# First scan: the remainders of 27 filler weight tiles on VectorE instead of GpSimd, their rounding some units ahead

## The chip, the cores and the metric

One core of one Trainium2 chip runs the whole program. The metric is the device time in microseconds (us) of one execution. In the text TensorE is PE in the profile, VectorE is DVE, ScalarE is ACT, GpSimd is POOL and SyncE is SP (its DMA queue SPq).

## What is computed

One inference step of one hybrid decoder layer: 2048 prompt tokens, 32 sample tokens, width 1024. In the part that matters here, normalised rows go through the input weight (1024 x 3072), and the pieces of the result feed a recurrence (HGRN2) in chunks and a gated chunk mixer:

```python
z = hn @ w_in
zq, zf, zi, zg, zu, zv = jnp.split(z, ...)
f = lb + (1.0 - lb) * jax.nn.sigmoid(zf32)
k = (1.0 - lb) * jax.nn.sigmoid(-zf32)
S_new, o = hgrn2_scan(S0, q, k, logf, v)        # per chunk, 4 heads
o_hg = rmsnorm_per_head(o) * jax.nn.sigmoid(zg)
u = jax.nn.gelu(zu)
vn = layernorm(jax.nn.gelu(zv), ln_v_g, ln_v_b)
o_cm = chunk_gmlp(u, vn, w_s, b_s)
x = x + jnp.concatenate([o_hg, o_cm], axis=-1) @ w_out
```

Cross-attention to 256 memory tokens and an MLP of width 4096 follow. All is float32.

## The kernel before

**Products.** A float32 product is made of three products of a rounded type (fp32r): each operand is split into a rounded part (`hi`) and a remainder (`lo`), and `gemm` (line 946) issues lo x hi, hi x lo and hi x hi. Activations are split by ScalarE (`a_hi`) and VectorE (`a_lo`), weights tile by tile.

**Blocks.** The prompt runs in four blocks of 512 tokens, "first" to "last". Weights come in tiles of 128x512 through a ring of RING = 8 pairs (`w_ring`: `w_hi`, `w_lo`). In the first block a tile is loaded raw (`w_raw`, RAW = 4 slots), split on the core, used, and its pair is stored to `w_pairs` in DRAM. The later blocks load ready pairs and split nothing. In the first block GpSimd splits most tiles by itself, two instructions each: rounding (line 864) and remainder (line 867), in `split`.

**The scan.** Tiles 0 to 23 of a block are zf, zi, zq. Then eight units (four chunks, two pairs of heads each) follow one another. For a unit u, TensorE issues the level products (`within_chunk`, line 1087), some tiles' products of zv, zg and zu as filler (`fill`, FILL = 5 ahead of the units, then 3, 2, 3, 2, 4, 3, 2), and the output and state products (`rows_and_state`, lines 1111 to 1113). Tiles 24 to 31 are zv, 32 to 39 zg, 40 to 47 zu, and 48 to 55 the first half of w_out, used behind the scan; two of these are used ahead of the transposes "oto" (line 954 in the profile), six behind them. After unit 6 come the chunk mixer's products "mix" (line 1155), which need zu's GELU and free halves of PSUM. PSUM is two halves of four banks; every job has one, and `begin` waits until the job before in that half is evacuated. zg and the outputs of units 4 to 7 share a half.

VectorE's order for unit u: `attention(u)` (needs the level products), `new_state(u - 1)` (line 2287), `args(u + 2)` (line 2238), `scaled(u + 1)` (end factors line 2246, then seven level products line 2251, which release `ends_ready` and `scaled_ready` for TensorE), then pieces of the layer norm by unit: statistics behind unit 1, scale behind unit 2, `lng_row` behind 3, `lnb_row` behind 4, `gate` behind 5, `uu` behind 6. In the first block `mixed_rows` stands behind all units, in the others behind unit 6; "oto" waits for the mixed rows.

ScalarE's order for unit u: `decays(u + 2)` (exponentials, lines 1640 to 1643), GELU of zv at u = 0, sigmoid of zg at u = 4 (SWAP, ahead of `decays(6)`), GELU of zu at u = 6 (all line 1708), the copies of the unit's output (`unit_out`), small square roots at u = 1 and 5, and then `filler_tiles(u)`. A change between kinds of function costs a table load (line 1431).

**Filler tiles.** FILLERS = (29, 56): the tiles 29 to 55 are rounded by ScalarE in `filler_tiles` (line 1673), at places given by FILLER_HI, and GpSimd makes each remainder (line 883) when its rounding is done. ScalarE waits, for tile i, for the store of the pair i - 8, the raw load of i, and TensorE's use of tile i - 8:

```python
act.wait_ge(w_stored[i % RING].sem, i // RING * 16 + 16)
act.wait_ge(w_in[i % RAW].sem, i // RAW * 16 + 16)
act.wait_ge(w_used.sem, W_TILES["mem"] + i + 1)
nc.scalar.copy(w_hi[:, i % RING, :], w_raw[:, i % RAW, :]).then_inc(filler_hi, 1)
```

**SyncE.** `load` (line 613) issues, tile after tile, the raw load of tile i (line 622) once the remainder of tile i - 4 is made (`w_split`), and then the store of pair i - 4 (line 604). `block_loads` (line 708) orders them: the six pieces of w_in (tiles 0 to 47), in the first block then `first_sample_loads` (49 small loads for the sample requests, lines 773 to 781, and two of 2 MB, line 757), then w_out's first half (tiles 48 to 55), a wait for unit 7's attention, the rows of x, and w_out's second half from tile 56 on.

The functions that the diff touches are printed below.

Of the kernel before, what the change touches and what calls it, by code (L numbers as in the profile page):

```python
# [17 lines left out]
ALU = mybir.AluOpType  # L18
# [34 lines left out]
FILL = (5, 3, 2, 3, 2, 4, 3, 2)  # L53

FILLERS = (29, 56)
FILLER_HI = {"zq": range(29, 33), "kt": range(33, 34), 0: range(34, 38), 1: range(38, 42), 2: range(42, 45), 3: range(45, 47), 4: range(47, 48),
             5: range(48, 52), 6: range(52, 56)}

SG = NS + DS
SLV = 3  # L60
# [146 lines left out]
def program(nc, I, O):  # L207
# [14 lines left out]
    with ctx:  # L222
# [630 lines left out]
        @block.gpsimd  # L853
        def _(pool):
            pool.sem_inc(w_split.sem, RAW)
            nc.gpsimd.memset(zero[:], 0.0).then_inc(w_rounded, 1)
            pool.wait_ge(w_rounded, 1)
            def split(g, k, n, tile0, by_act):

                s = k % RAW  # L860
                pool.wait_ge(w_stored[k].sem, g * 16 + (n // RING * 16 + 16))
                pool.wait_ge(w_in[s].sem, g * (16 * RING // RAW) + (n // RAW * 16 + 16 * (k // RAW + 1)))
                pool.wait_ge(w_used.sem, g * RING + (W_TILES["mem"] + tile0 + k + 1))
                nc.gpsimd.tensor_tensor(w_hi[:, k, :], w_raw[:, s, :], zero[:].to_broadcast([P, 512]),  # L864
                                        ALU.add).then_inc(w_rounded, 1)
                pool.wait_ge(w_rounded, g * RING + (n - by_act + k + 2))
                nc.gpsimd.tensor_tensor(w_lo[:, k, :], w_raw[:, s, :], w_hi[:, k, :].bitcast(F32),  # L867
                                        ALU.subtract).then_inc(w_split.sem, 1)

            for s in range(RING):  # L870
                pool.sem_inc(w_stored[s].sem, 16)
            first, after = FILLERS
            with pool.Fori(0, first // RING) as g:
                for k in range(RING):
                    if k % 4 == 0:
                        pool.wait_ge(*done("mem", ("nv", 5 if k == 0 else 7)))
                    split(g, k, 0, 0, 0)
            for i in range(first // RING * RING, first):
                split(0, i % RING, i // RING * RING, i // RING * RING, 0)
            for i in range(first, after):  # L880

                pool.wait_ge(filler_hi, i - first + 1)
                nc.gpsimd.tensor_tensor(w_lo[:, i % RING, :], w_raw[:, i % RAW, :], w_hi[:, i % RING, :].bitcast(F32),
                                        ALU.subtract).then_inc(w_split.sem, 1)
            with pool.Fori(0, (FOLD0 - after) // RING) as g:
                for k in range(RING):
                    split(g, k, after, after, after - first)
            with pool.Fori(0, (W_TILES["first"] - FOLD1) // RING) as g:
                for k in range(RING):
                    split(g, k, FOLD0, FOLD1, after - first)  # L890
# [533 lines left out]
        def _(act):  # L1424
# [207 lines left out]
            def block_scalar(pos, b, last):  # L1632
# [68 lines left out]
                for u in range(UNITS):  # L1701
                    if u + 2 < UNITS and u != SWAP:
                        decays(u + 2)
                    for at, name, dst in ((0, "zv", vn), (SWAP, "zg", gate), (6, "zu", uu)):
                        if u == at:
                            tables("sigmoid_and_others" if name == "zg" else "gelu_apprx_tanh_and_others")
                            act.wait_ge(*done(pos, name))
                            nc.scalar.activation(dst[:], out_of(pos, name)[:], ACT.Sigmoid if name == "zg" else
                                                 ACT.Gelu_apprx_tanh).then_inc(evacuated_of(pos, name), 1)
                    if u == SWAP:  # L1710
                        decays(u + 2)
                    if u == UNITS - 1:
                        round_hi_halves(pos, "otu", a_hi[:, 4:8, :])
                    unit_out(u)
                    if u == 1:
                        rsqrt(pos, "ln", TT)
                    if u == 5:
                        rsqrt(pos, "oa", 12)
                    filler_tiles(u)
                rsqrt(pos, "ob", 4)  # L1720
                round_hi(pos, "oto", a_hi[:, 0:4, :], out_of(pos, "oto")[:])
# [88 lines left out]
        def _(dve):  # L1810
# [420 lines left out]
            def block_vector(pos, last):  # L2231
# [11 lines left out]
                def scaled(u):  # L2243
# [7 lines left out]
                        ins = nc.vector.tensor_tensor(v, v, signed(kq, u, w), ALU.mult)  # L2251
                    ins.then_inc(scaled_ready.sem, 1)

                def attention(u):


                    ps = levels_of(pos, u)
                    wide = ps[:, 2, 0:2 * P].rearrange("p (j t) -> p j t", j=2)
                    v = ps[:, 3, 0:GROUP_LEVELS * 2 * GROUP].rearrange("p (a e j t) -> p a e j t", a=3, e=2, j=2)

                    def own_size(i, n=1):

                        return masks[:, i:i + n, None, 0:GROUP].bitcast(mybir.dt.int32).to_broadcast([P, n, 2, GROUP])

                    nc.vector.tensor_copy(yt[:, 36:37], ident[:, 0:1])
                    nc.vector.copy_predicated(v[:, :, 0], own_size(0, 3), v[:, :, 1]).then_inc(dve_sem, 1)
                    nc.vector.copy_predicated(att[:], masks[:, 5:6, :].bitcast(mybir.dt.int32).to_broadcast([P, 2, P]), wide)
                    dve.wait_ge(dve_sem, link.next())
                    nc.vector.tensor_copy(yt[:, 36:37], ident[:, 0:1])
                    nc.vector.copy_predicated(v[:, 0:1, 0], own_size(4), v[:, 1:2, 0]).then_inc(dve_sem, 1)  # L2270
                    dve.wait_ge(dve_sem, link.next())
                    nc.vector.tensor_copy(yt[:, 36:37], ident[:, 0:1])
                    nc.vector.copy_predicated(v[:, 0:1, 0], own_size(6), v[:, 2:3, 0]).then_inc(dve_sem, 1)
                    dve.wait_ge(dve_sem, link.next())
                    nc.vector.tensor_copy(yt[:, 36:37], ident[:, 0:1])
                    groups = [P, 2, P // GROUP, GROUP]
                    nc.vector.copy_predicated(att[:].rearrange("p j (g t) -> p j g t", t=GROUP),
                                              masks[:, 3:4, :].bitcast(mybir.dt.int32).rearrange(
                                                  "p j (g t) -> p j g t", t=GROUP).to_broadcast(groups),
                                              v[:, 0, 0, :, None, :].to_broadcast(groups)).then_inc(att_ready.sem, 1)  # L2280
# [43 lines left out]
                    "p h (c t) -> p h c t", c=TT), ALU.mult).then_inc(evacuated_of(pos, "zq"), 1)  # L2324
                dve.wait_ge(*out(pos, "zq"))
                scaled(0)
                for u in range(UNITS):
                    dve.wait_ge(levels_done.sem, levels_done.at(pos, u))
                    attention(u)
# [3 lines left out]
                        args(u + 2)  # L2333
                    if u + 1 < UNITS:
                        scaled(u + 1)
                    if u == 1:

                        dve.wait_ge(*out(pos, "zv"))
                        for t in range(TT):
                            ins = nc.vector.bn_stats(stats[:, t, :], vn[:, t, :])  # L2340
                        ins.then_inc(dve_sem, 1)
                        dve.wait_ge(dve_sem, link.next())
                        nc.vector.tensor_copy(yt[:, 36:37], stats[:, TT - 1, 0:1])
                        for t in range(TT):
                            ins = nc.vector.bn_aggr(mv[:, t, :], stats[:, t, :])
                        ins.then_inc(dve_sem, 1)
                        dve.wait_ge(dve_sem, link.next())
                        nc.vector.tensor_scalar(var[:, 16:16 + TT], mv[:, :, 1], EPS, None, ALU.add
                                                ).then_inc(var_ready.sem, 1)
# [26 lines left out]
                    if u == 6:  # L2376
                        dve.wait_ge(*out(pos, "zu"))
                        ps = out_of(pos, "mix")
                        for g in range(H):
                            c = slice(g * P, g * P + P)  # L2380
                            dve.wait_ge(mix_done.sem, mix_done.at(pos, g))
                            nc.vector.scalar_tensor_tensor(uu[:, :, c], ps[:, g, :].rearrange("p (t c) -> p t c", c=P),
                                                           bs_col[:, g:g + 1], uu[:, :, c], ALU.add, ALU.mult
                                                           ).then_inc(uu_ready.sem if g < H - 1 else
                                                                      evacuated_of(pos, "mix"), 1)
                if pos == "first":
                    mixed_rows()
                dve.wait_ge(o_ready.sem, o_ready.at(pos, UNITS - 1))
# [188 lines left out]
```

## Time and profile before

| | us |
|---|---|
| median of 3 runs | 2933.81 |
| lowest, highest | 2933.69, 2934.37 |
| profiled execution, its time | 2933.21 |
| profiled execution, its span | 2931.4 |
| TensorE busy | 2886.1 (98%) |
| weight loads (PEld) | 2334.1 (80%) |
| VectorE busy | 1251.3 (43%) |
| ScalarE busy | 642.9 (22%) |
| GpSimd busy | 440.9 (15%) |

The span runs from the first instruction to the last of the profiled execution; its time has 1.8 us around it. Shares of busy time are means over the whole span: the scans of the four blocks are short parts of it, in which the other engines set the pace at places. Times in the rows are counted from the span's start.

### The profile page before, as it was taken

Reading aid. Unit: us, or ns where it says so; the run is one execution under the profiler, and the core shown is the slowest. Engines: PE = TensorE matmul, PEld = TensorE weight load, DVE = VectorE, ACT = ScalarE, POOL = GpSimd, SP = SyncE. Lnnn points to the kernel's source line nnn. Section 1 sums busy time; section 2 is a strip of 40 time slices with the busy share of each in tenths; the row PEclk is TensorE's granted clock in tenths of the full one; section 3 lists DMA queues with packets and bytes.
Section 4 is the critical chain, followed back from the end, with each engine's and each line's share of the span. In section 5 each row is a group of like instructions: output and inputs, shape, how many; then the busy total and the mean of one; then the engine's idle time right before and its main releaser. Section 6 shows DMA issues by size and latency. Waiting matters only on the chain.

```text
span 2931.4 us, 40394 instructions
## 1 busy us (share of the span) xinstructions
PE 2886.1 (98%) x17243; PEld 2334.1 (80%) x17243; DVE 1251.3 (43%) x2096; ACT 642.9 (22%) x999; POOL 440.9 (15%) x362
## 2 busy tenths in 40 slices
PE   8998999999999999999999999999999999999998
PEld 7787787777888888788788888877778888877787
DVE  5578443453344733322243744222234473322233
ACT  4435221110123411111122422101012341211011
POOL 0182408788810000000000000000000000000000
PEclk9999999999999999999999999999999999999999
DMA  8895757989975455665666445566767545567654
GB/s 311 311 324 187 278 188 279 361 288 310 329 255 174 154 185 204 222 231 199 223 215 223 142 176 185 199 250 250 274 236 273 178 155 187 180 226 286 235 193 150
DMA packets 207677, 675.93 MB, mean 231 GB/s; under 512 B 22864, under 2 KB 28240, under 8 KB 207504
## 3 DMA queue, kind: packets, MB, share of 16 engines
q1 hardware_dynamic: 200480, 662.72, 63.3%
q10 hardware_dynamic: 7024, 10.68, 1.0%
q8 instruction: 136, 2.23, 0.3%
q14 instruction: 37, 0.30, 0.0%
HBM read 542.84 MB, written 130.48 MB: 230 GB/s over the span
## 4 chain that ended last, share of the span: by engine, by line
PE 89%; DVE 6%; SPq 1%; DMA 1%; ACT 1%; issue 0%; POOL 0%; ACTq 0%; DVEq 0%
PE half L946 81%; PE half L954 2%; PE half L1275 2%; DVE lvl L2238 1%; PE half L1087 1%; PE half L963 1%; DVE lvl L2251 1%; PE half L1155 1%; DMA w_raw<-in_w_out 0%; PE half L1285 0%; DMA mem_raw<-in_w_ck 0%; SPq L599 0%; DMA w_pairs<-stage 0%; DVE state L2287 0%; SPq L779 0%
## 5 line engine op out<-in xcount | busy, mean ns | idle before, releaser
L946 PE MATMUL half<-a_hi,w_ring 128*128 128x512 f32 x2560 | 822.6, 397 | 0.0
L946 PE MATMUL half<-w_ring,a_hi 128*128 128x512 f32 x2176 | 677.1, 392 | 0.0
L946 PE MATMUL half<-w_ring,ht_hi 128*128 128x512 f32 x2016 | 626.5, 392 | 0.0
L946 PEld LDWEIGHTS half<-a_hi,w_ring 128*128 128x128 f32 x2560 | 480.2, 188 | 131.6 <-issue 14.3
L946 PE MATMUL half<-a_lo,w_ring 128*128 128x512 f32 x1280 | 505.4, 395 | 0.0
L946 PEld LDWEIGHTS half<-w_ring,a_hi 128*128 128x128 f32 x2176 | 410.3, 189 | 90.0
L946 PEld LDWEIGHTS half<-w_ring,ht_hi 128*128 128x128 f32 x2016 | 378.9, 188 | 82.2
L946 PE MATMUL half<-w_ring,a_lo 128*128 128x512 f32 x1088 | 433.6, 399 | 5.1 <-DVE a_lo L1839 3.6
L946 PE MATMUL half<-w_ring,ht_lo 128*128 128x512 f32 x1008 | 395.5, 392 | 0.8 <-DVE ht_lo L2464 0.8
L2472 DVE SCALAR_TENSOR_TENSOR x<-half,rstd,x 128x512 f32<-128x512 f32 x252 | 171.7, 744 | 300.7 <-PE half L946 300.7
L946 PEld LDWEIGHTS half<-a_lo,w_ring 128*128 128x128 f32 x1280 | 240.2, 188 | 56.2
L946 PEld LDWEIGHTS half<-w_ring,a_lo 128*128 128x128 f32 x1088 | 205.3, 189 | 51.4 <-issue 5.4
L864 POOL TENSOR_TENSOR w_ring<-w_raw,zero 128x512 fp32r<-128x512 f32 x165 | 184.3, 1117 | 295.9 <-DMA w_raw<-in_w_up 129.0
L867 POOL TENSOR_TENSOR w_ring<-w_raw,w_ring 128x512 fp32r<-128x512 f32 x165 | 224.3, 1360 | 12.9
L946 PEld LDWEIGHTS half<-w_ring,ht_lo 128*128 128x128 f32 x1008 | 189.4, 188 | 44.3 <-DVE ht_lo L2464 1.3
L1760 ACT ACTIVATE relu<-half 128x2048 f32<-128x2048 f32 x32 | 60.3, 1883 | 660.5 <-PE half L946 654.4
L2461 DVE TENSOR_TENSOR relu<-relu,half 128x2048 f32<-128x2048 f32 x32 | 73.2, 2287 | 292.6 <-ACT relu L1760 292.6
L946 PE MATMUL half<-w_ring,b_hi 128*128 128x512 f32 x512 | 158.9, 392 | 0.0
L1461 ACT ACTIVATE a_hi<-half 128x2048 fp32r<-128x2048 f32 (+1 forms) x30 | 54.8, 1825 | 439.7 <-PE half L954 439.7
L1839 DVE TENSOR_TENSOR a_lo<-half,a_hi 128x2048 fp32r<-128x2048 f32 (+1 forms) x30 | 66.6, 2220 | 197.6 <-ACT a_hi L1461 197.6
L946 PEld LDWEIGHTS half<-w_ring,b_hi 128*128 128x128 f32 x512 | 96.2, 188 | 21.1
L2464 DVE TENSOR_TENSOR ht_lo<-relu,ht_hi 128x2048 fp32r<-128x2048 f32 x32 | 75.9, 2372 | 63.2 <-ACT ht_hi L1762 63.2
(309 smaller groups left out, 2473.6 us busy)
## 6 DMA issues: line engine op xcount, KB each, us to landing
w_ring<-w_pairs SPq DMA_DIRECT2D x704, 512.0 KB, 3.2
w_pairs<-w_ring SPq DMA_DIRECT2D x192, 512.0 KB, 5.0
w_pairs<-stage SPq DMA_DIRECT2D x16, 1024.0 KB, 6.0
w_raw<-in_w_up SPq DMA_DIRECT2D x64, 256.0 KB, 4.5
w_raw<-in_w_down SPq DMA_DIRECT2D x64, 256.0 KB, 3.9
w_s<-in_w_up SPq DMA_DIRECT2D x8, 2048.0 KB, 11.1
w_s<-in_w_down SPq DMA_DIRECT2D x8, 2048.0 KB, 11.5
w_raw<-in_w_in SPq DMA_DIRECT2D x48, 256.0 KB, 4.3
```

The source lines that it names most:

```text
L864: nc.gpsimd.tensor_tensor(w_hi[:, k, :], w_raw[:, s, :], zero[:].to_broadcast([P, 512]), ALU.add).then_inc(w_rounded, 1)
L867: nc.gpsimd.tensor_tensor(w_lo[:, k, :], w_raw[:, s, :], w_hi[:, k, :].bitcast(F32), ALU.subtract).then_inc(w_split.sem, 1)
L946: m = nc.tensor.matmul(ps[:, j, :], l, r, start=(i == 0 and q == 0), stop=(i == tiles_in - 1 and q == 2))
L954: m = nc.tensor.transpose(ps[:, bank0 + i // 4, (i % 4) * P:(i % 4) * P + P], t, ident[:])
L963: m = nc.tensor.matmul(out, l, r, start=(first and i == 0), stop=(last and i == 2))
L1275: m = nc.tensor.matmul(ps[rows, 0, :], src[:, k, :], w_s[k // 4][:, k % 4, c * 512:c * 512 + 512], start=(k < 2), stop=(k >= KD - 2))
L1461: nc.scalar.activation(dst, src, ACT.Copy, scale=scale).then_inc(hi_ready.sem, 1)
L1760: nc.scalar.activation(relu[:], out_of(pos, ("up", e))[:], ACT.Relu).then_inc(relu_ready.sem, 1)
L1839: ins = nc.vector.tensor_tensor(dst, src, hi.bitcast(F32), ALU.subtract)
L2461: nc.vector.tensor_tensor(relu[:], relu[:], out_of(pos, ("up", e))[:], ALU.mult).then_inc(sq_ready.sem, 1)
L2464: nc.vector.tensor_tensor(ht_lo[e % 2][:], relu[:], ht_hi[e % 2][:].bitcast(F32), ALU.subtract).then_inc(evacuated_of(pos, ("up", e)), 1)
L2472: ins = nc.vector.scalar_tensor_tensor(xc, out_of(pos, ("dn", e, c))[:, t, :], rstd[:, 24 + t:25 + t], xc, ALU.mult, ALU.add)
```

## The change

The remainders of the tiles 29 to 55 are made by VectorE, in eight groups (FILLER_LO): one behind scaled(0), one behind each scaled(1) to scaled(6), and the last behind all units, ahead of `mixed_rows`. GpSimd waits until they are made, and goes on with tile 56. FILLER_HI has ScalarE round the tiles at earlier places: 33 to 36 ahead of unit 0, then behind the units 0 to 5 37-39, 40-43, 44-45, 46-48, 49-51 and 52-55. The table for GELU is loaded behind unit 5's square root. SyncE's program is not changed.

```diff
-FILLER_HI = {"zq": range(29, 33), "kt": range(33, 34), 0: range(34, 38), 1: range(38, 42), 2: range(42, 45), 3: range(45, 47), 4: range(47, 48),
-             5: range(48, 52), 6: range(52, 56)}
+FILLER_HI = {"zq": range(29, 33), "kt": range(33, 37), 0: range(37, 40), 1: range(40, 44), 2: range(44, 46), 3: range(46, 49),
+             4: range(49, 52), 5: range(52, 56)}
+FILLER_LO = ((29, 33), (33, 37), (37, 40), (40, 44), (44, 46), (46, 49), (49, 52), (52, 56))
...
-            for i in range(first, after):
-
-                pool.wait_ge(filler_hi, i - first + 1)
-                nc.gpsimd.tensor_tensor(w_lo[:, i % RING, :], w_raw[:, i % RAW, :], w_hi[:, i % RING, :].bitcast(F32),
-                                        ALU.subtract).then_inc(w_split.sem, 1)
+            pool.wait_ge(w_split.sem, w_split.at("first", after - 1))
...
                     if u == 5:
                         rsqrt(pos, "oa", 12)
+                        tables("gelu_apprx_tanh_and_others")
                     filler_tiles(u)
...
+                def remainders(turn):
+
+                    for i in range(*FILLER_LO[turn]) if pos == "first" else ():
+                        dve.wait_ge(filler_hi, i - FILLERS[0] + 1)
+                        if i == FILLERS[0]:
+                            dve.wait_ge(w_split.sem, w_split.at(pos, i - 1))
+                        nc.vector.tensor_tensor(w_lo[:, i % RING, :], w_raw[:, i % RAW, :], w_hi[:, i % RING, :].bitcast(F32),
+                                                ALU.subtract).then_inc(w_split.sem, 1)
...
                 scaled(0)
+                remainders(0)
                 for u in range(UNITS):
...
                     if u + 1 < UNITS:
                         scaled(u + 1)
+                        if u + 1 < UNITS - 1:
+                            remainders(u + 1)
...
+                remainders(UNITS - 1)
                 if pos == "first":
                     mixed_rows()
```

## Rows read from the trace of the kernel before

**Rows 1.** Windows table, both scans: us, PE, PEld, DVE, ACT, POOL busy, PEclk, DMA, GB/s

```profile
215.60:278.50 62.90, 54.34 (x785) 44.66 (x785) 56.84 (x147) 36.49 (x76) 18.93 (x14) 0.97 0.48 169
278.50:313.90 35.40, 31.63 (x499) 27.72 (x497) 26.59 (x65) 18.13 (x41) 12.09 (x9) 0.95 0.80 303
...
2318.20:2372.00 53.80, 52.37 (x786) 43.58 (x785) 47.55 (x147) 29.24 (x62) 0.00 (x0) 1.00 0.40 138
2372.00:2402.80 30.80, 30.14 (x500) 26.28 (x499) 25.09 (x79) 12.97 (x32) 0.00 (x0) 1.00 0.32 113
```

**Rows 2.** The timeline of TensorE, first block: start us, us, instruction xcount [idle before]

```profile
303.75 5.31 PE L1155 MATMUL half<-vn,ws_t 128*128 128x128 f32 x32 [3.66 <-ACT uu L1708]
...
321.62 1.97 PE L954 MATMUL half<-ident,vv 128*128 128x128 f32 x16 [1.91 <-DVE vv L2295]
```

**Rows 3.** The timeline of TensorE, last block

```profile
2394.10 3.81 PE L1155 MATMUL half<-vn,ws_t 128*128 128x128 f32 x32 [0.50 <-ACT uu L1708]
...
2408.39 1.91 PE L954 MATMUL half<-ident,vv 128*128 128x128 f32 x16
```

**Rows 4.** The waits of TensorE, 215 to 325 us: total, times, longest

```profile
PE half L1111 <- issue: 3.8, 2, 2.3
...
PE half L1111 <- DVE ends L2246: 3.5, 1, 3.5
```

**Rows 5.** VectorE's groups by shape, first block's scan (207.8 to 321.7 us)

```profile
L2251 DVE TENSOR_TENSOR lvl<-lvl,kq 128x256 f32<-128x256 f32 x56 | 27.7, 561 | 0.0
L2238 DVE TENSOR_TENSOR lvl<-bn 128x256 f32<-128x256 f32 x42 | 19.4, 530 | 0.0
L2287 DVE SCALAR_TENSOR_TENSOR state<-state,e_last,added 128x128 f32<-128x128 f32 x16 | 10.4, 690 | 0.0
```

**Rows 6.** VectorE's groups by shape, last block's scan (2308.6 to 2408.5 us)

```profile
L2251 DVE TENSOR_TENSOR lvl<-lvl,kq 128x256 f32<-128x256 f32 x56 | 20.1, 432 | 0.0
L2238 DVE TENSOR_TENSOR lvl<-bn 128x256 f32<-128x256 f32 x42 | 15.0, 431 | 0.0
...
L2287 DVE SCALAR_TENSOR_TENSOR state<-state,e_last,added 128x128 f32<-128x128 f32 x16 | 4.9, 346 | 0.4 <-ACT osq L1663 0.4
```

**Rows 7.** Line 883 on GpSimd: durations ns min/median/max, first and last start

```profile
L883 POOL TENSOR_TENSOR w_ring<-w_raw,w_ring x27: 1267/1337/1692, 208.7 to 309.4; 128x512 fp32r<-128x512 f32 x27
```

**Rows 8.** The timeline of SyncE's queue, 258 to 280 us

```profile
258.98 0.33 SPq L622 DMA_DIRECT2D w_raw<-in_w_in  x1
...
278.74 0.95 SPq L757 DMA_DIRECT2D w_s<-in_w_in  x2
...
279.74 0.50 SPq L622 DMA_DIRECT2D w_raw<-in_w_out  x1
```

**Rows 9.** DMA issues at 278.74 and 279.74: KB each, us from issue to landing

```profile
w_s<-in_w_in SPq DMA_DIRECT2D x2, 2048.0 KB, 11.6
...
w_raw<-in_w_out SPq DMA_DIRECT2D x1, 256.0 KB, 14.5
```

**Rows 10.** The timeline of ScalarE, first block's scan

```profile
267.20 1.13 ACT L1673 CAST w_ring<-w_raw 128x512 fp32r<-128x512 f32 x2
...
270.46 1.89 ACT L1708 ACTIVATE gate<-half 128x2048 f32<-128x2048 f32 x1 [0.83 <-PE half L946]
...
294.28 0.63 ACT L1673 CAST w_ring<-w_raw 128x512 fp32r<-128x512 f32 x1 [0.30 <-DMA w_raw<-in_w_out]
...
300.43 1.28 ACT L1431 ACT_TABLE_LOAD   x1
```

**Rows 11.** The timeline of VectorE, first block, unit 6's scalings

```profile
296.62 0.68 DVE L2246 TENSOR_TENSOR ends<-ends,kq 128x512 f32<-128x512 f32 x1
297.22 5.75 DVE L2251 TENSOR_TENSOR lvl<-lvl,kq 128x256 f32<-128x256 f32 x7
```

**Rows 12.** The timeline of VectorE, last block, behind attention(2)

```profile
2343.35 0.61 DVE L2287 SCALAR_TENSOR_TENSOR state<-state,e_last,added 128x128 f32<-128x128 f32 x2
...
2346.90 2.51 DVE L2251 TENSOR_TENSOR lvl<-lvl,kq 128x256 f32<-128x256 f32 x7
```

## The prediction

> **What bounds the kernel now.** I read the page first: TensorE is busy for 98% of the span, so only its idle and slow-clock stretches can give time back or grow. The change touches the first block's scan alone, so I set that scan beside the last block's, which issues the same products with weights already split and has no filler tiles. The windows table cuts both at the same places: unit 0's level products, unit 4's output products, the first w_out product [rows 1]. The first block takes 62.9 and 35.4 us, the last 53.8 and 30.8: 13.7 us lost. To the transposes of "oto" it is 321.62 - 215.6 = 106.0 against 2408.39 - 2318.2 = 90.2, so 15.8 us is all that a perfect cure could return [rows 1, 2, 3]. The reader should see in rows 2 how the late part is lost: "mix" waits 3.66 us for ACT's GELU of zu and then runs 5.31 us where the last block's takes 3.81 after a 0.50 us gap; the granted clock averages 0.95 in that stretch, that is, a part of it ran at 1.2 GHz instead of 2.4. So a gap of some 3.5 us costs another 1.5 us behind it.
>
> The early part is lost on DVE [rows 4]: TensorE waits 3.5 us for the second unit's end factors and 3.8 us where the profile names nobody. The DVE groups by shape show why: scalings, arguments and state updates take 27.7, 19.4 and 10.4 us here, 20.1, 15.0 and 4.9 in the last block [rows 5, 6]. That is 17.5 us more for the same 114 instructions, and GpSimd's 27 remainders, 1.337 us each, run between them [rows 7].
>
> The third reading decides. SyncE issues tile 47's load at 258.98, as soon as GpSimd has the remainder of 43. Then come all the sample requests' small loads and two 2 MB loads (278.74), and only then tile 48, the first of w_out (279.74) [rows 8]. It lands 14.5 us after its issue, behind the 4 MB [rows 9]. ACT rounds it at 294.28, having waited for that DMA [rows 10]. From the remainder of 43 to the rounding of 48 is 294.28 - 258.98 = 35.3 us, and nothing in it depends on who makes remainders.
>
> **The change, part by part.** *Remainders leave GpSimd*: the 17.5 us of slowed DVE work go. *They come to DVE*: 27 of 128x512. The nearest DVE row is the end factors' 128x512 product, 296.62 to the next start at 297.22, 0.60 us [rows 11]; bounds are 0.36 (2.51 / 7, for half the size [rows 12]) and GpSimd's 1.337 [rows 7]. I take 0.60, as both its inputs lie in SBUF too: 27 x 0.60 = 16.2 us. On DVE's books the exchange is nearly even, 17.5 for 16.2. The Trainium skill (SBUF — State Buffer, "Who interferes with whom") says that a DVE instruction with two SBUF inputs blocks against a GpSimd one that reads SBUF; Perfetto Trace Analysis, "Optimizing Scalar/DVE Operations", also of the Trainium skill, adds that moving work between those two "might not help". Rows 5 to 7 agree with the first; the second alone would forecast about no change, and is my second case below.
>
> Turns 0 and 1 lie in DVE's wait for level products and cost nothing; without that cover they would cost 4 x 0.60 = 2.4 us each. Turns 2 and 3 lie ahead of attention(2) and of attention(3), where DVE is what TensorE waits for.
>
> *ACT rounds earlier*: FILLER_HI now has 46, 47 and 48 behind unit 3's output, where it had 45 and 46. SyncE's order is unchanged, so tile 48 still needs its 35.3 us after the remainder of 43. When is that? In the last block attention(2) is over at 2343.35, and scaled(3)'s seven products start at 2346.90 and take 2.51 [rows 12]: over at 2349.4, in the first block's time (2318.2 - 215.6 = 2102.6 less) 246.8. Add turn 2 (three tiles, 1.8, ahead of attention(2)) and turn 3 (four, 2.4): the remainder of 43 is ready at 251.0, 8.0 us sooner than the 258.98 of now. Tile 48 then can be rounded at 294.28 - 8.0 = 286.3. ACT reaches it after unit 3's output, near 266 to 268 (its casts of 45 and 46 start at 267.20 now [rows 10]). It waits there about 19 us, and its queue is in order.
>
> *What is queued behind that wait*: the sigmoid of zg, decays(6), unit 4's copies. TensorE's unit 4 output products write the half that zg holds, so they wait for this sigmoid. After the last cast the table load and the sigmoid take 270.46 + 1.89 - (267.20 + 1.13) = 4.0, less the 0.8 waited for TensorE, 3.2 us [rows 10]. So 286.3 + 0.6 + 3.2 = 290.1, against 278.5 now [rows 1]: **+11.6 us**. DVE waits too, for tile 48 in turn 5, with the addition of lnb_row and attention(5) behind it; both are wanted only after unit 4's output, so that costs nothing more. TensorE itself would be ready near 269.4 + 1.8 + 2.4 = 273.6, so it idles some 16 us. The earlier stretches' gains and losses all end in this gap.
>
> *From there to the first w_out product*: the w_out tiles now have long landed, so no GELU wait: the last block's 30.8, plus 0.6 because the cast of 55 needs the slot freed by TensorE's last filler product and stands ahead of zu's GELU, plus 1.5 for the slow clock behind the long gap: 32.9 against 35.4, **-2.5 us**. The GELU table load moved into unit 5 costs nothing: it runs ahead of ACT's wait for TensorE's last filler product; uncovered it is 1.28 us [rows 10].
>
> *To the "oto" transposes*: before, 321.62 - 313.9 = 7.7 us, 1.91 of it waiting for DVE's mixed rows [rows 2]. Turn 7 now stands ahead of those rows: 4 x 0.60 = 2.4 us in full. The gap becomes 4.3 us, long enough for another 1.5 us at the lower clock: **+3.9 us**.
>
> Tile 56's load now waits for the remainder of 52, and GpSimd's own splitting with it. Tile 56 is wanted six tiles after "oto"; two tiles take 7.7 - 1.9 = 5.8 us, so that is 17 us on, and a delay of 3 us stays hidden. Behind the scan the first block has no TensorE wait that could take back a shift, so it reaches the end whole.
>
> **Sum**: 11.6 - 2.5 + 3.9 = +13.0 us. The profiled execution took 2933.21, so 2946.2; the median of the three runs is 0.6 above it, so I forecast 2946.8. The only size that a page prices differently is the landing: by SBUF — State Buffer of the Trainium skill, "The DMA setup-cost knee", a transfer is about 2 us plus bytes at 436 GB/s, 12.2 us for the 4.46 MB from 278.74 on; the rows show 15.5 (294.28 - 278.74), so the page would make the sum some 3 us smaller, and the trace decides.
>
> **Rivals.** *A, forecast: tile 48 stalls ACT.* For it: an unchanged SyncE program and a measured 35.3 us. *B, not slower: the landing does not gate.* If tile 48 lands before 273.6 - 3.8 = 269.8, ACT's wait costs nothing. That needs 19 us instead of 35.3, for example if the small loads issued far faster than their 20 us or the 4 MB didn't stand ahead; the change is even already where the 35.3 are 13.0 less, 22.3. Then: the last block's 90.2, plus turns 2 to 4 in DVE's way (nine tiles, 5.4), 0.6 for the cast of 55, 2.4 for turn 7, about 2.0 because the first block's mixed rows stand behind unit 7, 1.5 of clock: 102.1 against 106.0, -3.9, 2929.9. *C, faster: B, and the remainders all fit into DVE's idle time*: the full 15.8, 2918.0. Against it: turn 7 sits right on the path. *D, a longer stall*: each DVE remainder at 1.0 us moves tile 48 by 7 x 0.4 = 2.8, and the clock stays low longer: 2951 to 2953. *E, DVE is not freed* because its slow instructions come from elsewhere than GpSimd: the 17.5 us are 2.2 a unit, so three units bring the remainder of 43, and the stall, 6.6 later: 2953.4. Rows 5 and 6 speak against it.
>
> **How the numbers follow.** A with D and E 0.87, B 0.10, C 0.03. 0.2% is 5.9 us, about what a measurement tells from no change. A and its variants lie above it at all but the low end, B within, C beyond: slower 0.86, same 0.11, faster 0.03. Range: down 8.2 for a landing 2 us sooner, no clock cost (3.0), half of turn 7 hidden (1.2) and 2 more for an earlier remainder of 43; up 6.3 by D and E: 2938.6 to 2953.1.
>
> **What would show it.** Right: one TensorE gap of about 16 us at unit 4's output products released by ACT's gate; an ACT idle of about 19 us ahead of one cast, released by the DMA of in_w_out; scaled lvl products at 432 ns mean; a GELU gap at "mix" under 2 us; a gap of some 4 us ahead of "oto"; no GpSimd work between 205 us and the first tile of the next group. Wrong: tile 48's cast without a wait, or DVE products still above 500 ns.

## The result: 20 us slower, and the profile after

| | before | after |
|---|---|---|
| median (runs) | 2934.09 (4) | 2954.22 (4) |
| lowest, highest | 2933.69, 2935.55 | 2953.15, 2957.27 |
| ratio, 95% interval | | 1.0067 [1.0055, 1.008] |
| profiled execution, time and span | 2933.21, 2931.4 | 2953.15, 2951.4 |
| TensorE, VectorE, GpSimd busy | 2886.1, 1251.3, 440.9 | 2888.0, 1253.4, 405.9 |

The changed kernel is slower, as forecast, by 20.1 us where 13.0 were forecast; its median lies 1.1 us above the upper end of the range. The busy sums tell nothing of it: TensorE's and VectorE's hardly moved. The waits do. This is the table of TensorE's waits in the changed kernel, 215 to 345 us (total, times, longest), which answers to [rows 4]:

```profile
PE half L1108 <- ACT gate L1705: 18.4, 1, 18.4
PE half L951 <- DVE vv L2302: 7.9, 1, 7.9
PE half L1108 <- DVE ends L2244: 3.2, 1, 3.2
PE half L1152 <- ACT uu L1705: 1.1, 1, 1.1
```

One gap of 18.4 us stands at unit 4's output products (line 1108), released by the sigmoid that reads zg. A second of 7.9 us stands ahead of "oto" (line 951), where [rows 2] had 1.91. The wait for GELU at "mix" fell from 3.66 to 1.10. The changed kernel's windows table, cut at the places of [rows 1], with a third stretch from the first w_out product to "oto":

```profile
215.40:293.30 77.90, 54.77 (x786) 44.86 (x785) 57.23 (x163) 34.42 (x73) 0.00 (x0) 0.89 0.62 227
293.30:326.20 32.90, 31.61 (x499) 27.74 (x499) 23.57 (x67) 20.65 (x46) 0.00 (x0) 0.95 0.35 125
326.20:339.80 13.60, 5.72 (x24) 4.37 (x24) 12.86 (x30) 3.00 (x9) 4.56 (x4) 0.78 0.99 369
```

The first stretch has 77.9 us instead of 62.9 with the same products, the second 32.9 instead of 35.4, the third 13.6 instead of 7.7. The column behind ACT, GpSimd's, holds nothing for two stretches and four instructions in the third: these four matter below.

Next, the cause of the large gap. ScalarE's timeline in the changed kernel (start us, us, instruction, idle before it):

```profile
266.42 0.62 ACT L1670 CAST w_ring<-w_raw 128x512 fp32r<-128x512 f32 x1 [2.16 <-PE half L943]
289.36 0.62 ACT L1670 CAST w_ring<-w_raw 128x512 fp32r<-128x512 f32 x1 [22.32 <-DMA w_raw<-in_w_out]
290.00 1.28 ACT L1428 ACT_TABLE_LOAD   x1
291.29 1.88 ACT L1705 ACTIVATE gate<-half 128x2048 f32<-128x2048 f32 x1
```

The cast of tile 48, now the third behind unit 3's output, waits 22.32 us for its load; the table load and zg's sigmoid stand behind it in the queue, and TensorE goes on at 293.31, when the sigmoid is over. Now why the load is late: SyncE's queue in the changed kernel,

```profile
249.07 0.33 SPq L623 DMA_DIRECT2D w_raw<-in_w_in  x1
...
250.40 1.01 SPq L605 DMA_DIRECT2D w_pairs<-w_ring  x1
251.46 0.50 SPq L623 DMA_DIRECT2D w_raw<-in_w_in  x1
252.00 1.15 SPq L605 DMA_DIRECT2D w_pairs<-w_ring  x1
253.19 0.64 SPq L623 DMA_DIRECT2D w_raw<-in_w_in  x1
253.87 1.19 SPq L605 DMA_DIRECT2D w_pairs<-w_ring  x1
255.09 0.89 SPq L774 DMA_DIRECT2D own<-in_c_own  x1
...
274.74 0.95 SPq L758 DMA_DIRECT2D w_s<-in_w_in  x2
275.74 0.50 SPq L623 DMA_DIRECT2D w_raw<-in_w_out  x1
```

and the same place in the kernel before:

```profile
258.98 0.33 SPq L622 DMA_DIRECT2D w_raw<-in_w_in  x1
259.35 0.73 SPq L604 DMA_DIRECT2D w_pairs<-w_ring  x1
260.12 0.46 SPq L773 DMA_DIRECT2D own<-in_c_own  x1
```

One line of VectorE's timeline of the changed kernel shows when the four remainders 40 to 43 were made:

```profile
248.37 2.49 DVE L2258 TENSOR_TENSOR w_ring<-w_raw,w_ring 128x512 fp32r<-128x512 f32 x4
```

They are over by 250.86 (248.37 + 2.49), but the load of tile 47 is issued at 253.19 and the first sample load at 255.09. The four remainders arrive 0.6 us apart; each lets SyncE issue a load and a store, and its eight DMAs take 6.0 us. From the remainder of 43 to the first sample load it is 4.23 us, where it was 1.14 (260.12 - 258.98). The sample loads and the two of 2 MB then take 20.65 us (19.62 before), and tile 48 is cast 13.62 us behind its issue (14.54 before): 38.5 us in all, where [rows 8, 10] gave 35.3. Of the 3.2 more, 3.1 stand in that first part, 1.0 in the small loads, and the landing is 0.9 shorter.

VectorE was freed as said. Its groups by shape in the changed kernel, first block's scan, which answer to [rows 5] and [rows 6]:

```profile
L2249 DVE TENSOR_TENSOR lvl<-lvl,kq 128x256 f32<-128x256 f32 x56 | 20.0, 428 | 0.0
L2258 DVE TENSOR_TENSOR w_ring<-w_raw,w_ring 128x512 fp32r<-128x512 f32 x27 | 17.0, 683 | 16.6 <-ACT w_ring L1670 16.6
L2236 DVE TENSOR_TENSOR lvl<-bn 128x256 f32<-128x256 f32 x42 | 15.0, 431 | 0.0
```

The 56 scalings take 20.0 us instead of 27.7, the 42 arguments 15.0 instead of 19.4: the last block's figures. The new 27 remainders take 17.0. VectorE's 16.6 us of idleness is its own wait for tile 48, and costs nothing more.

Last, the gap at "oto". VectorE in the changed kernel:

```profile
334.44 1.00 DVE L1824 SCALAR_TENSOR_TENSOR yt<-y 128x4 f32<-128x4 f32 x1 [0.51 <-ACT y L1438]
335.48 0.16 DVE L1827 TENSOR_TENSOR yt<-yt,var 128x4 f32<-128x4 f32 x1
335.68 1.11 DVE L1829 SCALAR_TENSOR_TENSOR rstd<-yt,y 128x4 f32<-128x4 f32 x1
336.83 2.96 DVE L2302 SCALAR_TENSOR_TENSOR vv<-vv,rstd,gate 128x128 f32<-128x128 f32 x4
```

VectorE in the kernel before, the same instructions:

```profile
319.84 0.16 DVE L1826 SCALAR_TENSOR_TENSOR yt<-y 128x4 f32<-128x4 f32 x1 [0.51 <-ACT y L1441]
...
320.43 1.14 DVE L2295 SCALAR_TENSOR_TENSOR vv<-vv,rstd,gate 128x128 f32<-128x128 f32 x4
```

Two of the three little ones take 1.00 and 1.11 us instead of 0.16, and the four products 2.96 instead of 1.14. What runs beside them is GpSimd, in the changed kernel:

```profile
334.39 1.04 POOL L865 TENSOR_TENSOR w_ring<-w_raw,zero 128x512 fp32r<-128x512 f32 x1 [129.77 <-DMA w_raw<-in_w_out]
335.50 1.27 POOL L868 TENSOR_TENSOR w_ring<-w_raw,w_ring 128x512 fp32r<-128x512 f32 x1
```

and in the kernel before:

```profile
322.60 1.04 POOL L864 TENSOR_TENSOR w_ring<-w_raw,zero 128x512 fp32r<-128x512 f32 x1 [11.91 <-DMA w_raw<-in_w_out]
```

Before, GpSimd took up tile 56 at 322.60, when the mixed rows were made (320.43 + 1.14 = 321.57). After, turn 7 has pushed the mixed rows back by 2.5 us, while tile 56 comes in nearly as early: 8.2 us behind the first w_out product (334.39 - 326.17) against 8.6 (322.60 - 313.96). They meet.

### The profile page after: what moved, and what is told of

It is laid out like the page before. It is cut to its first block, busy times and chain, and to the rows that moved or that the text cites. A ratio compares the mean times of both kernels' runs of the same rounds, so it can differ in the third digit from the quotient of the medians.

```text
span 2951.4 us, 40395 instructions
## 1 busy us (share of the span) xinstructions
PE 2888.0 (98%) x17243; PEld 2335.9 (79%) x17243; DVE 1253.4 (42%) x2123; ACT 643.3 (22%) x999; POOL 405.9 (14%) x335
## 4 chain that ended last, share of the span: by engine, by line
PE 89%; DVE 6%; DMA 2%; SPq 1%; ACT 1%; issue 0%; ACTq 0%; DVEq 0%
PE half L943 80%; PE half L951 2%; PE half L1272 2%; DVE lvl L2249 1%; DVE lvl L2236 1%; PE half L1084 1%; PE half L960 1%; DMA w_raw<-in_w_out 1%; PE half L1152 1%; PE half L1282 0%; DMA mem_raw<-in_w_ck 0%; SPq L600 0%; SPq L780 0%; DVE stats L2350 0%; DMA w_pairs<-stage 0%
```

## The experiments

The profiled executions differ by up to 4 us ahead of the first block's scan, which the change doesn't touch. So besides the time each has a *stretch*: from unit 0's key transposes (starts 213.1 to 217.0) to the first product of the sample requests' part (line 1272 of the changed kernel). It is 494.06 - 215.32 = 278.7 us before and 514.28 - 215.17 = 299.1 after: 20.4 of difference, the whole change. Behind that point the two kernels take the same time to 0.2 us (2437.3 and 2437.1 of their spans); the kernels of the experiments take 2436.3 to 2441.0, with no edit there, so a difference of this size in a span is no effect of an edit. Each stretch is read from one execution, and a single time is weaker still: next to the experiments 5 to 8 the kernel before ran once too, and took 2940.60, 6.5 us over its usual median. What is said below of the experiments 1, 2 and 5 to 8 therefore rests on their stretches and rows, and nothing on a stretch's last microsecond.

**1. Tile 48 alone one place later.** The changed kernel, with its cast and remainder behind unit 4's output.

```diff
-FILLER_HI = {... 3: range(46, 49), 4: range(49, 52), 5: range(52, 56)}
-FILLER_LO = (... (46, 49), (49, 52), (52, 56))
+FILLER_HI = {... 3: range(46, 48), 4: range(48, 52), 5: range(52, 56)}
+FILLER_LO = (... (46, 48), (48, 52), (52, 56))
```

> The changed kernel with one place of one tile undone: tile 48 is rounded behind unit 4's output instead of unit 3's, and its remainder goes from VectorE's turn 5 to turn 6. Theory (ScalarE, in order, holds zg's sigmoid behind the cast of tile 48): the cast still starts near 289.4, released by the DMA of in_w_out, but zg's sigmoid runs near 271, so the wait of 18.4 us ahead of unit 4's output products is gone and those products start near 275. ScalarE's wait now stands behind unit 4 and holds decays(7) and unit 5's copies, so TensorE loses a part again ahead of unit 6's output products (6 to 8 us). The span falls by 8 to 11 us from 2951.4, to 2941 to 2944. Rival (VectorE, with 27 remainders more, is what TensorE waits for): the gap stays at 12 us or more, released by VectorE, and the span falls by less than 3 us.

Measured: 2944.71 in one run, stretch 289.1, 10.1 us less than after. TensorE's waits:

```profile
PE half L1108 <- DVE ends L2244: 12.2, 2, 9.0
```

The gap at unit 4 is gone, so it is tile 48's place that makes it. But the load is no earlier: the cast waits until 291.89, now with decays(7) queued behind, and 9.0 us of gap return at unit 6's output, where 6 to 8 were expected. Moving a wait down a queue gave back half of it.

**2. GpSimd held until the mixed rows are made.** The changed kernel with one wait more:

```diff
             pool.wait_ge(w_split.sem, w_split.at("first", after - 1))
+            pool.wait_ge(mixed_ready.sem, mixed_ready.at("first", TT - 1))
```

> The changed kernel, with GpSimd held from tile 56 on until the mixed rows are done. Theory (the mixed rows of the changed kernel run into GpSimd's resumed splitting): the last four updates of the mixed rows take 1.1 us in sum as in the kernel before, not 2.96, the two small steps ahead of them 0.16 each instead of 1.0 and 1.1, and the gap ahead of the oto transposes falls from 7.9 to 4.3 us; the span falls by 3.6 us, to about 2948, up to 2 us more if the clock then stays at its upper level. Rival (the gap is long because VectorE's own queue is longer: remainders and rows): the gap stays within 1 us of 7.9 and the span within 1 us.

Measured: 2949.79 in one run, stretch 296.1 (3.0 less, where the gap alone is 3.6 shorter). VectorE's timeline of this kernel ahead of "oto", and then TensorE's at it:

```profile
335.62 1.14 DVE L2303 SCALAR_TENSOR_TENSOR vv<-vv,rstd,gate 128x128 f32<-128x128 f32 x4
```

```profile
336.82 1.54 PE L952 MATMUL half<-ident,vv 128*128 128x128 f32 x6 [4.31 <-DVE vv L2303]
```

With GpSimd out of the way the products take 1.14 again and the gap is 4.31 us, the prediction's 4.3. The other 3.6 us of the gap are the collision.

**3 and 4. The sample requests' loads behind w_out's first half**, in the changed kernel (3) and in the kernel before (4).

```diff
-                if pos == "first":
-                    first_sample_loads()
                 load(pos, 6 * KD, I["w_out"][0], 0, 0, (4, 5, 6, 7, 0, 1, 2, 3))
+                if pos == "first":
+                    first_sample_loads()
```

> The changed kernel, with the sample requests' loads (49 small ones and the two of 2 MB) issued behind the loads of the tiles 48 to 55 instead of ahead of them. Theory (those loads set the time of tile 48): ScalarE waits for tile 48 at most 2 us, TensorE's gap at unit 4's output products is under 1 us, they start near 275, and the span falls by 17 to 19 us, to 2932 to 2935. Rival (VectorE is the bound behind it): TensorE still waits 4 us or more in the units 4 to 6, now for VectorE, and the span stays above 2938.

> The kernel before, with the same move of the sample requests' loads. Theory: the wait of 3.7 us ahead of the mixer's products for the GELU of zu, and the 1.5 us at the lower clock behind it, go, since tile 48 no longer keeps ScalarE; the span falls from 2931.4 by 3 to 5 us, to 2926.5 to 2928.5. Rival (the loads only move their price to the rows of x and the second half of w_out, which then come 10 us later): TensorE waits for those tiles or the sum with x, and the span rises by 2 us or more.

Measured for 3: median 2930.74 of 10 runs against 2935.04 of 16 of the kernel before, ratio 0.9985 [0.9975, 0.9994]; stretch 275.7, 23.4 less than after, more than the 17 to 19 expected. In ScalarE's timeline of this kernel tile 48's cast now waits for TensorE, for the 2.5 us that any filler cast there waits:

```profile
271.36 0.62 ACT L1670 CAST w_ring<-w_raw 128x512 fp32r<-128x512 f32 x1 [2.47 <-PE half L943]
```

TensorE's waits have no line for the gate any more, and "oto" leads them:

```profile
PE half L951 <- DVE vv L2302: 4.3, 1, 4.3
```

GpSimd takes up tile 56 at 332.64, 14.6 us behind the mixed rows (over at 318.06), since its load is now queued behind the sample loads: the collision is gone too, without the wait of experiment 2. The collision's 3.6 us are a part that the expectation had left out.

Measured for 4: median 2942.05 of 7 runs, ratio 1.0024 [1.0013, 1.0036], that is 7.0 us more; stretch 289.0, 10.2 more than before's one profiled execution. The wait at "mix" is gone as hoped, but see TensorE's waits and GpSimd's timeline of this kernel:

```profile
PE half L946 <- POOL w_ring L867: 10.2, 1, 10.2
```

```profile
298.89 1.73 POOL L883 TENSOR_TENSOR w_ring<-w_raw,w_ring 128x512 fp32r<-128x512 f32 x1
...
342.33 1.04 POOL L864 TENSOR_TENSOR w_ring<-w_raw,zero 128x512 fp32r<-128x512 f32 x1 [33.29 <-DMA w_raw<-in_w_out]
```

GpSimd makes the last remainder that w_out's first half waits for at 300.6 (298.89 + 1.73). Only then can the 49 small loads and the 4 MB be issued, from 302.57 on; tile 56 follows at 326.53, and TensorE waits 10.2 us for it behind "oto". Up to "oto" kernel 4 is 2.6 us ahead of the kernel before (103.7 against 106.3 from the key transposes); behind it it loses 12.8, these 10.2 and what the granted clock of 0.50 from 342.00 to 352.00 adds. In kernel 3 the small loads begin at 292.08 and tile 56's load is issued at 315.79. So the same edit of SyncE's order pays with the changed kernel's earlier fillers and costs with the old ones; I had expected a gain in both.

**5. The new places alone, GpSimd still makes the remainders**: the kernel before with the change's FILLER_HI and its table load behind unit 5's square root, nothing else.

> The kernel before with the rounding places (and the GELU table place) of the change alone; GpSimd still makes all 27 remainders. Theory (the loss is in when ScalarE meets tile 48, not in who makes remainders): ScalarE waits 15 us or more for the DMA of in_w_out ahead of the cast of tile 48, TensorE waits 12 to 16 us ahead of unit 4's output products for zg's sigmoid, which start at 287 to 291, and the span rises from 2931.4 by 7 to 12 us, to 2938 to 2943. Rival (the remainders on VectorE make the loss, by burdening the engine that TensorE waits for): no gap over 4 us in the scan, and the span stays within 2 us of 2931.4.

Measured: 2948.62 in one run, stretch 290.8 (12.0 more than before). TensorE's waits:

```profile
PE half L1111 <- ACT gate L1708: 12.1, 1, 12.1
PE half L1111 <- DVE ends L2247: 5.1, 1, 5.1
PE half L954 <- DVE vv L2296: 1.9, 1, 1.9
```

The gate's gap is there with GpSimd's remainders: the stall, and 12.0 of the 20.4 us, belong to where the tiles are rounded, not to who subtracts. The other 8.4 come only with the remainders on VectorE: from the key transposes to unit 4's output products it is 75.3 us here and 78.1 after, from there to "oto" 41.4 and 46.5, behind it 174.1 and 174.4. Here the "oto" gap is the old 1.9. Two lines, of SyncE and of ScalarE in this kernel, explain the first 2.9:

```profile
253.17 0.82 SPq L622 DMA_DIRECT2D w_raw<-in_w_in  x1
```

```profile
287.81 0.62 ACT L1673 CAST w_ring<-w_raw 128x512 fp32r<-128x512 f32 x1 [15.61 <-DMA w_raw<-in_w_out]
```

GpSimd, at 1.3 us and more for each, lets the load of tile 47 go at 253.17, with the first small load 1.37 us behind it, and tile 48 is cast 34.6 us later: about the 35.3 of the kernel before, and not the 38.5 of the changed one. From the key transposes its remainder of 43 is 1.0 us later than VectorE's (36.7 against 35.7), and tile 48's cast is still 2.9 earlier (71.3 against 74.2). The span rose by 15.4, 3.4 us more than the stretch, and past the 2938 to 2943 expected; 1.2 of them lie ahead of the stretch (216.47 for 215.32), and 2.2 behind its end, inside the spread given above.

**6. Only the two 2 MB loads moved**, in the changed kernel, behind w_out's first half; the 49 small ones stay.

```diff
 def first_sample_loads(): ...
-                load_product("zqf")
 ...
                 load(pos, 6 * KD, I["w_out"][0], 0, 0, (4, 5, 6, 7, 0, 1, 2, 3))
+                if pos == "first":
+                    load_product("zqf")
```

> The changed kernel with only the two 2 MB loads issued behind the loads of the tiles 48 to 55; the small ones stay where they are. Theory (of the 38.4 us between tile 43's remainder and tile 48's rounding about 24 are SyncE's issuing and the rest is landing behind 4 MB): tile 48's load is issued near 274.7 as before and lands 3 us later, its cast starts near 278, and the gap ahead of unit 4's output products is 6 to 8 us instead of 18.4; the span falls by 9 to 12 us, to 2939.5 to 2942.5. Rival (the 4 MB are all of it, the issue overlaps): the cast starts before 270 and the gap is gone. Rival (the small loads keep the DMA rings as busy as the large ones): the cast stays near 289.

Measured: 2940.96 in one run, stretch 288.4 (10.7 less than after). ScalarE and SyncE of this kernel:

```profile
276.15 0.62 ACT L1671 CAST w_ring<-w_raw 128x512 fp32r<-128x512 f32 x1 [11.23 <-DMA w_raw<-in_w_out]
```

```profile
272.88 0.36 SPq L623 DMA_DIRECT2D w_raw<-in_w_out  x1
```

Tile 48 is cast 3.27 us behind its issue, where it was 13.62: the 4 MB ahead of it were some 10 us of the wait. What is left, 24.2 us from the remainder of 43 (248.73) to the issue, is SyncE's issuing alone, and TensorE still waits 7.3 us for the gate.

**7. Turn 7 earlier.** The changed kernel with its last four remainders ahead of `uu`, instead of ahead of the mixed rows.

```diff
                     if u == 6:
+                        remainders(UNITS - 1)
                         dve.wait_ge(*out(pos, "zu"))
...
-                remainders(UNITS - 1)
                 if pos == "first":
                     mixed_rows()
```

> The changed kernel with turn 7 (tiles 52 to 55) ahead of the mixer's updates in unit 6, in VectorE's wait for the mixer's products, instead of ahead of the mixed rows. Theory: the 2.4 us come off the path to the oto transposes, and the mixed rows are over before GpSimd resumes, so that the 3.6 us of the collision go too: the gap falls from 7.9 to about 1.9 us and the span by 6 to 8 us, to 2943.5 to 2945.5. Rival (GpSimd resumes earlier as well, because tile 52's remainder is made earlier, and still collides): the gap falls by 2.4 alone, to 5.5, and the span to about 2949.

Measured: 2946.66 in one run, stretch 293.1 (6.0 less than after). The "oto" gap is 1.90 us and the mixed rows' products take 1.14. This takes both shares of that gap away, turn 7's 2.4 and the collision's 3.6: 6.0.

**8. Remainders 42 and 43 later**, in the changed kernel: behind the scale of the layer norm, so that SyncE gets two and two.

```diff
-                            remainders(u + 1)
+                            remainders(u + 1, (40, 41) if u == 2 else None)
...
                         ins.then_inc(dve_sem, 1)
                         dve.wait_ge(dve_sem, link.next())
+                        remainders(3, (42, 43))
```

> The changed kernel, with the remainders of 42 and 43 made behind the layer norm's scaling instead of ahead of it, 2.5 us later. Theory (in the changed kernel SyncE's back-to-back issues, not the remainder of 43, set the time of the sample requests' loads: the remainder was made at 250.9, the load of tile 47 issued at 253.2): the load of tile 47 is issued at 253.5 to 254.3, tile 48's cast starts within 1 us of 289.4, and the span stays within 1 us of 2951.4. Rival (the remainder of 43 sets it one to one): the cast starts near 291.9 and the span rises by 2.5 us.

Measured: 2954.08 in one run, stretch 300.3 (1.2 more). This is the test of the back-to-back issuing. VectorE of this kernel, then its SyncE:

```profile
251.17 1.29 DVE L2258 TENSOR_TENSOR w_ring<-w_raw,w_ring 128x512 fp32r<-128x512 f32 x2
```

```profile
251.89 0.33 SPq L623 DMA_DIRECT2D w_raw<-in_w_in  x1
...
252.77 1.34 SPq L623 DMA_DIRECT2D w_raw<-in_w_in  x1
...
254.92 0.48 SPq L774 DMA_DIRECT2D own<-in_c_own  x1
```

Counted from the key transposes (214.26 here, 215.17 after), the remainder of 43 is made at 38.2 instead of 35.7, 2.5 us later, and yet tile 48 is cast at 74.23 against 74.19. So a remainder of 43 made 2.5 us later costs tile 48 nothing. In the changed kernel the load of tile 47 goes only 2.33 us behind that remainder (253.19 - 250.86), since SyncE is still busy with the DMAs of the ones before it; here SyncE has had a pause ahead of 251.89, and the load goes 0.31 us behind (252.77 - 252.46). Counted from the key transposes it is issued 0.5 us later than in the changed kernel and the first small load 0.7 later, and the small loads take 0.6 less. The 1.2 us of the stretch lie between unit 4's output products and "mix", 0.7 of them in a longer wait there (1.76 for 1.10).

**9. Three edits together**: the changed kernel with the edits of 3, 7 and 2.

> The changed kernel with three edits together: the sample requests' loads behind those of the tiles 48 to 55 (as in the run with those alone), turn 7 in VectorE's wait for the mixer's products, and GpSimd held until the mixed rows are done. Theory: each edit takes its own term, so the scan has no gap at unit 4's output products, the gap ahead of the oto transposes falls from 4.3 to about 1.9 us, and the clock stays at its upper level behind it; from unit 0's key transposes to the first sample product it is 275.7 - 3.9 = about 272 us, against 278.8 in the kernel before, and the time is 0.2 to 0.3% under the kernel before. Rival (VectorE's waits in the units 2 and 3, or tile 56, which GpSimd now starts later, take the place of what is removed): that stretch stays at 275 us or more and the time within 0.15% of the kernel before.

Measured: median 2928.27 of 11 runs against 2934.79 of 15 of the kernel before, ratio 0.9976 [0.9967, 0.9985]; stretch 273.6, between the 272 of the theory and the 275 of its rival. It is faster than both kernels. Two of its TensorE waits, 205 to 520 us:

```profile
PE half L944 <- POOL w_ring L868: 2.1, 2, 1.2
PE half L952 <- DVE vv L2303: 1.9, 1, 1.9
```

It is 2.1 us less than in kernel 3. The "oto" gap gives 2.4 back and the transposes behind it another 1.35 (1.97 instead of 3.32), and TensorE waits 2.1 us in all for GpSimd's first tiles, tile 56 landing only at 331.31: the rival that looked to tile 56 holds in part. The added wait on the mixed rows holds nothing here, since that load lands long after them.

## What the prediction had right, and the two steps that failed

The time came out above the range. The direction and the mechanism of the stall were right; two steps of the sum failed, and they make 6.8 of the 7.3 us by which it is short (20.3 - 13.0).

**Tile 48 stalls ScalarE: right, and shown.** Experiment 1 takes the tile from there and the gate's gap goes; experiment 3 takes away what delays the load and it goes too; experiment 5 has it, of 12.1 us, without VectorE's remainders. The rival in which the landing does not gate has fallen; experiment 3 is what it would have been, 3.0 us shorter than before in the stretch, near its -3.9.

**The freed VectorE and the price of a remainder: right.** The remainder of 43 was forecast for 251.0 and was ready at 250.86; four of them take 2.49 us, 0.62 each for the 0.60 of the forecast. The rival in which VectorE is not freed (E, 2953.4) has fallen by the groups, and the one of dearer remainders (D, 1.0 us each, 2951 to 2953) by that price. Their times lie nearest to the measured 2954.2, but by luck: what they name did not happen. The advice of the Trainium skill (Perfetto Trace Analysis, "Optimizing Scalar/DVE Operations") that such a move "might not help" is right for VectorE's own books here (17.5 us gone, 17.0 come), but says nothing of the 20 us, which come from the order of the queues.

**The term that was mis-sized first: the 35.3 us from the remainder of 43 to the rounding of 48.** It was taken over with the words that nothing in it depends on who makes remainders. That step failed. It depends on how they arrive: GpSimd made them 1.3 us and more apart, and SyncE kept up; VectorE makes four in 2.5 us, and SyncE needs 6 us for their eight DMAs. 38.5 us instead of 35.3: +3.2, and the products at 293.31 instead of 290.1. Experiment 5, with GpSimd's remainders at the same places, has 34.6, and experiment 8 splits the four in two, and tile 48 is cast no later for it. The forecast had allowed for a longer stall only through dearer remainders.

**To the first w_out product: right.** 326.17 - 293.31 = 32.9, as forecast, and so are its parts: the wait for GELU is 1.10, the last block's 0.50 and the 0.6 for the cast of tile 55, and a granted clock of 0.59 over 3.7 us is worth 1.5.

**The term that was mis-sized second: the "oto" gap.** Turn 7's 2.4 us on top of 1.91 were right, as experiment 2 shows (4.31). What failed is the sentence that tile 56's delay stays hidden. It asked only when TensorE wants the tile, not what VectorE does when GpSimd starts on it; the exchange of slowed VectorE work that the first reading had found in [rows 5, 7] was not applied to this place. 7.92 instead of 4.3: +3.6. The Trainium skill's rule (SBUF — State Buffer, "Who interferes with whom"), that a VectorE instruction with two SBUF inputs contends with a GpSimd one that reads SBUF, fits the collision: the slowed VectorE instructions have two inputs in SBUF, and GpSimd reads `w_raw` there. Read at this place, it would have warned of it.

**Clock: 1.5 us forecast, 2.0 measured.** From "oto" to the first sample product it is 514.28 - 339.84 = 174.4 us, before 494.06 - 321.62 = 172.4. The transposes alone take 3.67 us instead of 1.97.

The sum in the forecast's own steps: 13.0 + 3.2 + 3.6 + 0.5 = 20.3, against 514.28 - 494.06 = 20.2 measured. Landing (SBUF — State Buffer of the Trainium skill, "The DMA setup-cost knee"): by the page's formula an estimate of 12.2 us was worked out for what is issued from 278.74 on, where the row gave 15.5; in the changed kernel it is 289.36 - 274.74 = 14.6. The rows differ from the estimate by 2.4 and 3.3 us, and they decide. The windows table has 339 GB/s for 274.70 to 289.40 in the changed kernel, where the formula has 436.

**Not settled**: what makes the part behind the stretch differ by up to 4.7 us between kernels (2436.3 to 2441.0), and the gap of 3.2 us at unit 3 (the products at 258.73 wait for the end factors), 2.7 to 3.2 in every version of the changed kernel and 2.3 in the kernel before. VectorE works without a pause from the four remainders at 248.37 to these end factors (over at 258.63), so turn 3's 2.5 us lie in that chain; no run took them out.

## What to carry to other kernels

Before work is moved earlier in an in-order queue, look for what it waits on that doesn't move with it, and for what stands behind it; a moved wait has to be tested together with the order of loads that feeds it, for the same reorder was worth 23 us on one side of this change and -10 on the other by the stretches, 24 and -7 by the medians. A measured delay between two events may be carried over only if the rate at which the first ones arrive is the same. When an engine is idled for a while, ask not only when it is late but what it runs beside when it comes back.

## What the runs showed of the hardware

**Issuing slows when DMAs follow closely.** A load after a pause takes SyncE 0.33 us to issue. In the changed kernel's run of eight, the stores take up to 1.19, the later loads 0.50 and 0.64, and the first small one behind them 0.89. The kernel before slows too: with GpSimd's remainders 1.3 us apart its stores from 245.68 on take 0.55, 0.79, 1.04 and 1.26, and SyncE just keeps up. Whether the close issue or the traffic still in flight does it no run separates: behind the two loads of 2 MB a load of 256 KB takes 1.20 us to issue (277.98). The 49 small loads together hold the queue for 19.7 us (274.74 - 255.09).

**The collision with GpSimd hits the smallest instructions hardest.** A VectorE instruction of 128x4 went from 0.16 to 1.00 and 1.11 us, about the time of the GpSimd instruction beside it (1.04 and 1.27), while its neighbour at 335.48, issued before GpSimd's second began at 335.50, kept its 0.16. VectorE's instruction waits for the end of GpSimd's rather than sharing with it. In four kernels the first of the three starts at a different point of GpSimd's 1.04 us, and always ends 0.01 to 0.03 us behind it:

| | GpSimd ends | VectorE's starts | takes | ends |
|---|---|---|---|---|
| after | 335.43 | 334.44 | 1.00 | 335.44 |
| experiment 1 | 326.50 | 325.71 | 0.81 | 326.52 |
| experiment 6 | 322.41 | 321.56 | 0.88 | 322.44 |
| experiment 8 | 335.66 | 334.74 | 0.94 | 335.68 |

**The granted clock after a gap.** In the changed kernel the windows table has 0.59 for TensorE from 293.30 to 297.00, behind the 18.4 us, and 1.00 from there; it has 0.50 from 339.80 to 344.00, behind the 7.9 us, that is the 1.2 GHz level. But the length of the gap just before doesn't decide. With the same 1.90 us of idleness ahead of "oto", experiment 7 ran the transposes behind it at 0.62 and experiment 9 at 1.00:

```profile
333.70:337.00 3.30, 3.25 (x18) 3.15 (x19) 0.00 (x0) 0.20 (x1) 2.60 (x3) 0.62 1.04 415
```

```profile
314.10:317.50 3.40, 3.34 (x23) 3.08 (x24) 0.01 (x1) 1.33 (x1) 0.00 (x0) 1.00 1.02 422
```

The stretches ahead of both are at 1.00. What tells them apart no run shows; the 0.5 us by which the clock's term was off stays without a cause.
